# Hybrid decoder block: part of the first modulation summed by column products, and tile 1 of x moved to a later load

## What is computed

```python
c_act = jax.nn.silu(c)
mod = (c_act @ w_ada[l] + b_ada[l])[:, None, :]
sh1, sc1, g1, sh2, sc2, g2 = jnp.split(mod, N_MOD, axis=-1)
h = rms_norm(h_res, norm1_g[l]) * (1.0 + sc1) + sh1
proj = h @ w_in[l]                       # q | k | v | u, width 1280
# q, k: QK-norm and partial rotary; sliding-window attention with sinks
# u: pooling mixer over windows of 2, 4, 8 and 16 positions
h_res = h_res + g1 * mixed
h2 = rms_norm(h_res, norm2_g[l]) * (1.0 + sc2) + sh2
ff = jnp.square(jax.nn.relu(h2 @ w_mlp_in[l])) @ w_mlp_out[l]
h_res = h_res + g2 * ff
```

## Time and profile before

| | us |
|---|---|
| median of 3 runs | 965.35 (964.99 to 967.53) |
| the profiled execution | 964.76 |
| its span between first and last instruction | 963.0 |
| PE busy | 923.1 |
| DVE busy | 656.4 |
| ACT busy | 491.4 |
| POOL busy | 348.6 |

### The profile page before, as it was taken

How to read it: one execution, slowest core, us unless ns; L and a number is a source line. 1 busy time by engine, 2 the same in 40 slices (tenths; PEclk the granted TensorE clock), 3 DMA queues, 4 the chain that set the end, 5 groups by cost and what they waited for, 6 DMA issues and landing times.

```text
span 963.0 us, 12639 instructions
## 1 busy us (share of the span) xinstructions
PE 923.1 (96%) x4411; PEld 762.8 (79%) x4411; DVE 656.4 (68%) x1000; ACT 491.4 (51%) x874; POOL 348.6 (36%) x342
## 2 busy tenths in 40 slices
PE   1899999998999999999999999999999999999998
PEld 1787788886778888788888788888888888888887
DVE  6976887878554587665566544535687666789896
ACT  1756677778465564645544455454343544333331
POOL 8041211116232443988788877851000000000000
PEclk9999999999999999999999999999999999999999
DMA  9852432214222240765456534548998837997772
GB/s 357 323 170 74 131 110 88 80 54 155 87 88 88 88 153 22 232 203 177 164 168 203 176 132 134 173 143 274 331 354 292 280 98 235 312 323 233 237 248 105
DMA packets 92271, 175.54 MB, mean 182 GB/s; under 512 B 9320, under 2 KB 26288, under 8 KB 92208
## 3 DMA queue, kind: packets, MB, share of 16 engines
q1 hardware_dynamic: 92096, 174.70, 54.0%
q10 hardware_dynamic: 112, 0.04, 0.0%
HBM read 136.95 MB, written 37.75 MB: 181 GB/s over the span
## 4 chain that ended last, share of the span: by engine, by line
PE 84%; DVE 7%; ACT 5%; issue 2%; DMA 1%; SPq 1%; POOL 0%; DVEq 0%; ACTq 0%
PE psum L1965 26%; PE psum L1967 26%; PE psum L1966 25%; PE psum L1961 3%; DMA slots<-in_w_ada 1%; ACT probs L777 1%; PE psum L2041 1%; ACT qT L796 1%; DVE squares L1162 1%; PE psum L2091 1%; PE psum L2022 1%; PE psum L2020 1%; PE psum L2019 1%; ACT probs L785 1%; PE psum L2064 1%
## 5 line engine op out<-in xcount | busy, mean ns | idle before, releaser
L1072 ACT CAST down_operands<-down_raw 128x1024 fp32r<-128x1024 f32 x96 | 100.9, 1054 | 152.5 <-PE psum L1967 57.6
L1965 PE MATMUL psum<-down_operands 128*128 128x512 f32 x448 | 174.3, 389 | 0.0
L1966 PE MATMUL psum<-down_operands 128*128 128x512 f32 x448 | 174.3, 389 | 0.0
L1967 PE MATMUL psum<-down_operands 128*128 128x512 f32 x448 | 174.3, 389 | 0.0
L1701 DVE TENSOR_TENSOR down_operands<-down_raw,down_operands 128x1024 fp32r<-128x1024 f32 x93 | 112.4, 1220 | 16.3 <-ACT down_operands L1072 15.4
L1965 PE MATMUL psum<-h2T,w_operands 128*128 128x512 f32 x272 | 107.4, 395 | 1.9 <-DVE act_quads_a L1645 1.3
L1967 PE MATMUL psum<-h2T,w_operands 128*128 128x512 f32 x272 | 106.0, 390 | 0.0
L1966 PE MATMUL psum<-h2T,w_operands 128*128 128x512 f32 x272 | 105.9, 389 | 0.0
L1917 POOL TENSOR_TENSOR w_operands<-raw,w_operands 128x512 fp32r<-128x512 f32 x56 | 83.1, 1485 | 42.2 <-ACT w_operands L1024 42.2
L1966 PEld LDWEIGHTS psum<-down_operands 128*128 128x128 f32 x448 | 84.1, 188 | 17.6
L1965 PEld LDWEIGHTS psum<-down_operands 128*128 128x128 f32 x448 | 84.1, 188 | 17.5
(11 more groups left out here) (249 smaller groups left out, 1965.5 us busy)
## 6 DMA issues: line engine op xcount, KB each, us to landing
down_raw<-in_w_mlp_out SPq DMA_DIRECT2D x160, 256.0 KB, 4.5
down_raw<-act_scratch SPq DMA_DIRECT2D x112, 256.0 KB, 3.4
raw<-in_w_ada SPq DMA_DIRECT2D x32, 512.0 KB, 4.5
raw<-in_w_mlp_in SPq DMA_DIRECT2D x32, 512.0 KB, 4.8
act_scratch<-act_quads_a SPq DMA_DIRECT2D x64, 256.0 KB, 2.3
act_scratch<-act_quads_b SPq DMA_DIRECT2D x48, 256.0 KB, 3.5
slots<-in_w_ada SPq DMA_DIRECT2D x8, 512.0 KB, 10.5
xh<-in_x SPq DMA_DIRECT2D x8, 512.0 KB, 5.8
```

The source lines that it names most:

```text
L1072: nc.scalar.copy(o[:, 0, :, :], r[:, 0:2, :]).then_inc(op2_hi, 1)
L1965: mm(o, wh, ah, start=first, stop=False, skip_group_check=adds)
L1966: mm(o, wh, al, start=False, stop=False, skip_group_check=adds)
L1967: return mm(o, wl, ah, start=False, stop=last, skip_group_check=adds)
```

## The change

- sc1 pieces 6 and 7 are no longer added by DVE (`SC1_DVE` is KD - 2, which is 6). PE multiplies them directly: `column_sum` takes 128 columns of the piece as the stationary operand and one column as the moving operand (silu for a raw piece, ones for a sum that DVE has made), which sums over the partitions and lands the result as one column of PSUM. acc is summed in that way too, and acc_sc (pieces 0 to 5), all of sc1 into the same PSUM columns. `turn_sums` and the three `TENSOR_REDUCE` go.
- Tile 1 of x is issued behind wu piece 1 instead of ahead of sc1, squared on ACT behind `hi_wu(1)`, scaled on GpSimd (`g.tensor_scalar` on `xh[:, 1, :]`) and turned behind `project_u(0)`.
- The six `keep_clock` products between the turns of x and of acc_sc go.
- The buffers of sc1 pieces 6 and 7 are given back by PE (`sc1_used`, `sc1_turned`).

```diff
@@ the buffers of sc1
-                eng.wait_ge(mod_summed, k + 1 + (KD if kind == "sc1" else 0) + (kind == "sc1" and k == KD - 1))
+                if kind == "sc1" and k == SC1_DVE:
+                    eng.wait_ge(sc1_used, 1)
+                elif kind == "sc1" and k == KD - 1:
+                    eng.wait_ge(sc1_turned, 2)
+                else:
+                    eng.wait_ge(mod_summed, k + 1 + (KD if kind == "sc1" else 0))
@@ SP
-                if n == 7:
+                if n == place[("sh1", KD - 1)]:
                     load_x(0)
+                if n == place[("wu", 1)]:
                     load_x(1)
@@ ACT
             square_x(0)
-            square_x(1)
             scale_x(0)
-            scale_x(1)
             hi_wu(0)
             hi_wu(1)
+            square_x(1)
             hi_h(0, 0)
@@ DVE
-            for n in range(2 * KD):
+            for n in range(KD + SC1_DVE):
...
-                    v.tensor_reduce(b1, banks(0).rearrange("p (k n) -> p k n", n=P), AX_X, ALU.add).then_inc(mod_taken, 1)
...
+                    v.tensor_tensor(b1.rearrange("p (h k) -> p h k", h=2), psum[:, 0:2, 0:4],
+                                    cols[:, 8 * SH1:8 * SH1 + 8].rearrange("p (h k) -> p h k", h=2),
+                                    ALU.add).then_inc(mod_taken, 1)
...
-                own_d.step(v.tensor_reduce(a1[:, c4], bank(2 + h).rearrange("p (k n) -> p k n", n=P), AX_X, ALU.add))
-                own_d.wait()
-                own_d.step(v.tensor_tensor(a1[:, c4], a1[:, c4],
+                own_d.step(v.tensor_tensor(a1[:, c4], psum[:, 2 + h, 0:4],
                                            cols[:, 8 * SC1 + 4 * h:8 * SC1 + 4 * h + 4], ALU.add))
@@ GpSimd
-            pool.wait_ge(x_squared, 2)
-            root(rx[:, 0:2], ssx[:, 0:2], D, x_root)
+            root_x(0)
+            root_x(1)
+            pool.wait_ge(x_root, 2)
+            g.tensor_scalar(xh[:, 1, :], xh[:, 1, :], rx[:, 1:2], None, ALU.mult).then_inc(x_scaled, 1)
@@ PE
+            def column_sum(at, n, a, by, first, last):
+                to = psum[:, at + n // 4, n % 4:n % 4 + 1]
+                return mm(to, a[:, n * P:(n + 1) * P], by, start=first and n % 4 == 0, stop=last, skip_group_check=True)
...
-            turn_sums(banks(0), acc).then_inc(mod_turned, 1)
+            for n in range(KD):
+                ins = column_sum(0, n, acc, ones[:, 0:1], True, True)
+            ins.then_inc(mod_turned, 1)
             pe.wait_ge(mod_summed, 2 * KD - 5)
             keep_clock(8, 2)
             turn_x(0)
-            pe.wait_ge(cols_ready, 1)
-            turn_x(1)
-            keep_clock(6, 2)
+            a = landed(pe, ("sc1", SC1_DVE))
+            for n in range(KD):
+                ins = column_sum(2, n, a, silu[:, SC1_DVE:SC1_DVE + 1], True, False)
+            ins.then_inc(sc1_used, 1)
+            pe.wait_ge(mod_summed, KD + SC1_DVE)
+            for n in range(KD):
+                column_sum(2, n, acc_sc, ones[:, 0:1], False, False)
+            a = landed(pe, ("sc1", KD - 1))
             for h in range(2):
-                pe.wait_ge(mod_summed, 2 * KD + h)
-                turn_sums(bank(2 + h), acc_sc[:, 512 * h:512 * h + 512]).then_inc(sc1_turned, 1)
+                for n in range(4 * h, 4 * h + 4):
+                    ins = column_sum(2, n, a, silu[:, KD - 1:KD], False, True)
+                ins.then_inc(sc1_turned, 1)
             pe.wait_ge(mod_taken, 1)
             keep_clock(14, 0)
 
             project_u(0)
+            turn_x(1)
```

More of the change, by code:

```diff
@@ L233, in build @@
         WO_POOL, WO_DVE = (0, 5, 6), (1, 2, 3, 4, 7)
+        SC1_DVE = KD - 2
         JOB_LOADS = (4, 4, 4, 3, 4, 4, 1, 0)
@@ L268, in build @@
         sc1_turned = sem("sc1_turned")
+        sc1_used = sem("sc1_used")
         mod_taken = sem("mod_taken")
@@ L704, in scale_x @@
             def scale_x(t):
-                act.wait_ge(x_root, max(t, 1))
+                act.wait_ge(x_root, t + 1)
                 nc.scalar.activation(xh[:, t % 2, :], xh[:, t % 2, :], ACT.Copy,
@@ L1195, in _ @@
                     add_piece(acc[:, :], ("sh1", n), n, mod_summed)
-                elif n < 2 * KD - 1:
+                else:
                     add_piece(acc_sc, ("sc1", n - KD), n - KD, mod_summed)
-                else:
-                    a = landed(dve, ("sc1", KD - 1))
-                    for h in range(2):
-                        cut = slice(512 * h, 512 * h + 512)
-                        v.scalar_tensor_tensor(out=acc_sc[:, cut], in0=a[:, cut], scalar=silu[:, KD - 1:KD],
-                                               in1=acc_sc[:, cut], op0=ALU.mult, op1=ALU.add).then_inc(mod_summed, 1)
                 if n == 4:
@@ L1206, in _ @@
                     v.tensor_copy(rows[64:72, :], posi[64:72, :]).then_inc(posf_ready, 1)
-                if n == KD + 2:
+                if n == KD - 1:
                     dve.wait_ge(rows_turned, 1)
                     v.tensor_copy(cols[:, :], psum[:, 4, 0:72]).then_inc(cols_ready, 1)
-                if n == 2 * KD - 4:
+                if n == KD + 4:
                     dve.wait_ge(cols_ready, 1)
                     dve.wait_ge(mod_turned, 1)
-                    v.tensor_reduce(b1, banks(0).rearrange("p (k n) -> p k n", n=P), AX_X, ALU.add).then_inc(mod_taken, 1)
-                    dve.wait_ge(mod_taken, 1)
-                    own_d.step(v.tensor_tensor(b1, b1, cols[:, 8 * SH1:8 * SH1 + 8], ALU.add))
+                    v.tensor_tensor(b1.rearrange("p (h k) -> p h k", h=2), psum[:, 0:2, 0:4],
+                                    cols[:, 8 * SH1:8 * SH1 + 8].rearrange("p (h k) -> p h k", h=2),
+                                    ALU.add).then_inc(mod_taken, 1)
             def scale_1(h):
                 c4 = slice(4 * h, 4 * h + 4)
+                if h == 0:
+                    dve.wait_ge(mod_taken, 1)
                 dve.wait_ge(sc1_turned, h + 1)
-                own_d.step(v.tensor_reduce(a1[:, c4], bank(2 + h).rearrange("p (k n) -> p k n", n=P), AX_X, ALU.add))
-                own_d.wait()
-                own_d.step(v.tensor_tensor(a1[:, c4], a1[:, c4],
+                own_d.step(v.tensor_tensor(a1[:, c4], psum[:, 2 + h, 0:4],
                                            cols[:, 8 * SC1 + 4 * h:8 * SC1 + 4 * h + 4], ALU.add))
```

## The result

| | median, us | runs | ratio to before [95%] |
|---|---|---|---|
| before | 965.32 (964.99 to 967.53) | 5 | |
| after | 972.78 (969.17 to 974.13) | 5 | 1.0066 [1.0054, 1.0078] |
| after once more | 973.88 (972.32 to 974.06) | 4 | 1.0078 [1.0063, 1.0093] |

The change loses 7.5 us. The forecast was 967.2, a loss of 1.9, and the range ended at 970.8. The forecast's likeliest case did not happen; its slower rival, TensorE at the lower clock level, did.

A forecast was written before the change was run, and what follows sets the result against it. PE, 96% busy, was bound by when it enters tile 0's projection, set by T plus 16.3 us of DVE work. T +2.5, reduction -0.65: +1.9 on 964.76 gives 966.7, median 967.2; range 963.0 to 970.8.

The forecast's parts named there:

- likeliest case: Late root of tile 0 with PE at its higher clock level: +0.5 to +2.8 us, chance 0.45.
- T: Start of make_h on DVE, 31.60 us before; forecast at 34.1 (33.3 to 34.1), a move of +2.5.
- L: End of DVE's last low part of the weights, 47.93 us before; forecast shift +1.9.
- Root late on POOL: DVE's additions hold small POOL instructions, so the root of tile 0 ends at 25.9 us, against 24.34 before.
- Price of the late root: Without DVE holding POOL, the root would be ready by 21.5 and the forecast sum 1.2 us less.
- Column products: On PE, 40 instructions ahead of a1's first half at 0.11 us: 4.4 us; bounds 2.4 and 9.2.
- Scaling of tile 1 on GpSimd: Begins at 32.2 us, takes 1.90; DVE's second small step of a1 ends with it, giving T = 34.1.
- Behind T: DVE's 16.3 us become 15.65 without the second reduction; turn of tile 1 on PE hidden, cover 0.8 us.
- Rival of the lower level: PE's clock stays low, products 0.17 to 0.23 us, T 36.0 to 38.4: +4.4 to +7, near 970.5; chance 0.22.
- Rival of the cheap products: Root in time on POOL, PE products at 0.11 us or less: 964.6 down to 962 us; chance 0.25.
- Rival of no move: Landing of the weights, not DVE's list, bounds the part behind T: 965.4 us; chance 0.08.

The follow-up runs named there:

- after once more: The changed kernel run again with nothing altered: 973.88 us, ratio 1.0078 to before.
- typical profile: Profile from the unchanged rerun of the changed kernel: span 972.0, time 973.71 us; that run's median is 973.88.
- filled: Changed kernel with keep_clock(18, 2) instead of keep_clock(8, 2), filling PE's pause ahead of the turn of tile 0; products still one column: 969.86 us, ratio 1.0045.
- first profile of after: Profile of the changed kernel's fastest execution of its first five: span 967.4, time 969.17 us.
- the square above: Medians of the changed kernel, late then early root of tile 0: one-column products 973.88 and 967.37 us; 128-column sc1 products 969.08 and 964.14 us.
- x1_only: Kernel before with only tile 1 of x moved (load, square, GpSimd scaling, turn), sums as before: 966.43 us, ratio 1.0008.
- wide_root: Changed kernel with the 24 sc1 products moving 128 columns and the root of tile 0 early on POOL: 964.14 us, ratio 0.9974.
- wide_root_act: Changed kernel with 128-column sc1 products and early root, tile 1 scaled on ACT behind hi_wu(3) instead of GpSimd: 963.87 us, ratio 0.9983.
- wide24: Changed kernel with the 24 products of sc1 moving 128 equal columns instead of one: 969.08 us, ratio 1.0033.
- root_early: Changed kernel with POOL making the root of tile 0 ahead of the fourth pooling window's constants: 967.37 us, ratio 1.0013.
- x1_act_fed: Kernel before with tile 1 moved but scaled on ACT, early root, and keep_clock(24, 0) instead of keep_clock(14, 0): 964.41 us, ratio 0.9979.

## Why the prediction was wrong

**The step that failed** is the term for the column products: 40 instructions at 0.11 us, 4.4 us, with the clock taken to be at its higher level. In the typical profile they run at the lower level, at 0.20 to 0.213 us, and take 8.4 us; PE's `keep_clock(14, 0)` behind them stays at the lower level too, so that the turn of tile 1, which the sum had hidden, comes 2.25 us late. The price is right for the higher level (0.106). What was wrong is that the level would stay. The prediction named this as its first rival and weighed one row against it: the turns at 29.78, at the higher level after 0.49 us of pause. That pause is much shorter than the 2.2 us that the prediction itself expected, and the row has no narrow product in it. PE was as busy as with `keep_clock`, 4.00 of 4.00 us in `filled`, and the clock fell all the same.

The forecast of T, 34.1, redone with what the typical trace shows: the turn starts 0.4 later than thought (27.50) and takes 1.76 instead of 0.9 us, the forty instructions take 8.4 instead of 4.4 us, and the small steps of DVE fall behind the scaling of tile 1 and are not held, which gives 1.06 back. 34.1 + 0.4 + 0.86 + 4.0 - 1.06 = 38.3; the trace has 38.29. So of the 7.1 us between the forecast shift of L (+1.9) and the measured one (+8.98), about 4.2 lie ahead of T and about 3 behind it.

Point by point:

- *Loads*: right. sc1 piece 0 was expected at 17.2; DVE takes it at 16.8 in the typical trace and at 17.8 in the other.
- *Root late on POOL*: the end of the root was right in the typical trace, 26.26 against the forecast 25.9, and so were the idle PE ahead of the turn (3.26 us, 2.2 forecast) and that DVE's additions hold small GpSimd instructions up. But that the number fits is luck in part. The count began with a memset at 18.4 and six instructions behind it, one per addition. In the typical trace that memset comes at 21.39, as the constants ahead of it were held up already; of the six behind it three were held and three slipped through once DVE was done:

```profile
21.57 0.90 POOL L1786 TENSOR_SCALAR_AFFINE_SELECT band<-band 128x16 f32<-128x16 f32 x1
...
25.70 0.56 POOL L1823 TENSOR_TENSOR small<-small 128x1 f32<-128x1 f32 x1
```

  In the first profile of after the memset comes at 18.20, as the prediction had it. There two selections slipped through around a pause of DVE (18.69 to 19.06) and the root ended at 24.73, not at 25.9. Timeline of POOL in that profile:

```profile
23.13 1.60 POOL L1823 TENSOR_TENSOR small<-small 128x1 f32<-128x1 f32 x1
...
32.85 2.86 POOL L1832 TENSOR_SCALAR xh<-xh,small 128x1024 f32<-128x1024 f32 x1
```

  The instruction that takes 1.60 us here takes 0.56 at 25.70 in the typical profile, when DVE is done with its additions. That is what the Trainium skill's "SBUF — State Buffer", section "SBUF: two separate sides", would have: whichever of the two starts first holds the shared ports for its whole length.
- *Price of the late root*: the square above gives 4.9 to 6.5 us. The prediction put it at 1.2 us, which doesn't follow from its own terms either: 2.2 us for the turn and 1.05 for the scaling, less up to 0.7 further on, is 2.5. It priced the delay alone, without what stands at the lower level behind it.
- *Column products*: the mechanism of the price (the weight load) was right, the size only for one level. The Trainium skill's "TensorE: Matmul & The Clock Gate", section "LDWEIGHTS (loading the stationary operand)", gives columns / 1.2 in ns, 107 ns here. The traces agree at the higher level (0.106) and not at the lower, where it is 0.213. The bounds 0.06 and 0.23 held both.
- *Scaling of tile 1 on GpSimd*: mis-sized, 2.86 us instead of 1.90. That it holds one of DVE's small steps was right where the two meet: 0.53 us in the first profile of after, 0.66 in `x1_only`, 0.83 in `wide_root`, against 0.16 in `wide_root_act`. That the step ends with the scaling was wrong. It ends 1.12 to 1.13 us behind the scaling's start in all three (33.98, 33.27 and 33.31, the scaling from 32.85, 32.14 and 32.18), with another 1.7 us of scaling to come, and the splitting of a weight, which has two inputs in SBUF, then runs at its usual 1.22 us beside it (33.38 in `x1_only`). So the rule of the whole length holds in these rows for GpSimd behind DVE and is not borne out for DVE behind GpSimd, unless the scaling's recorded length is too long; no run tells the two apart. Held to the end of the scaling, T in the first profile would be near 35.75. In the typical run they don't meet.
- *T in the first profile*, 34.02, agrees with the forecast 34.1 only by chance: the root was 1.2 us early there, the turn of tile 0 ran at the lower level (1.62 us instead of 0.9), and so did the last ten or so of the forty instructions.
- *Behind T*: wrong. From T to L 15.65 us were forecast; it is 17.25 in the first profile of after and 18.62 in the typical one. The removed reduction is there, but the turn of tile 1, said to be hidden with 0.8 us to spare, comes 0.9 and 2.25 us late (DVE reached it at 43.10 before, so 10.8 us behind T without the reduction and not 11.1: the cover was about 0.5 thin), and 0.6 us more are lost at the last low parts, half of it in a wait for an ACT high part. With wide products the cover holds: no such wait in `wide24` and `wide_root`, whose T to L is 15.83 and 16.39, the latter with the 0.83 us step in it.
- *Rival of the lower level*: this is what happened. It asked for products at 0.17 to 0.23 us and T at 36.0 to 38.4 (measured 0.20 to 0.213 and 38.29), and a sum of +4.4 to +7; measured +7.5. (Its T leaves out the 0.2 us ahead of DVE's steps that the sum has; with them it is 36.2 to 38.6.) It had a chance of 0.22, and the range was cut at 970.8, inside it. Its "another 1 us from the cover" was too little by its own terms: 28 instructions at 0.23 are 3.1 us longer than 3.3, and a cover of 0.8 leaves 2.3. Measured are waits of 2.07 to 2.32 us in the three traces where `keep_clock(14, 0)` takes 5.6 to 6.0 us (`root_early`, typical, `filled`).
- *Rival of the cheap products*: 0.06 us or below an instruction was seen nowhere; the lowest is 0.106.
- *Rival of no move*: excluded; the shift of L is the shift of the time in eight of the thirteen profiles, within 0.2 us, and the other five have more time at the lower clock.

What stays open: what made sc1 piece 0 come 1.0 us later, and POOL's last memset 3.2 us earlier, in one execution of after than in another, of which one pauses 3.26 us ahead of the turn and the other 0.46; and why the clock falls at some 225 to 240 us in some executions of several kernels only. In the first profile of after that fall comes behind two pauses of PE, of 1.11 and 0.72 us (PE is busy 1.16 of the 2.00 us from 226); before has such a pause too (0.89 of 2.00 us from 222) and no fall.

## What to carry to other kernels

An engine that the profile calls busy isn't yet one that keeps its clock. Where small TensorE products stand ahead of a critical stretch, price them at both clock levels, and price what stands behind them at the lower one too. Where such products are bound by their weight load anyway, let them move 128 columns instead of one: here that cost 0.112 instead of 0.106 us an instruction, and more room in PSUM, and the clock rose and stayed up. And a chain with time to spare (here the root on POOL) must be looked at again when a change puts the critical work behind it in the same queue.

## What was not expected of the hardware

- A column product in float32 costs 0.106 us an instruction at the higher level and 0.213 at the lower. With 128 moved columns it is 0.112 at the higher level.
- PE with 24 narrow products (48 instructions) in a row is busy without a gap, and the granted clock falls to 0.50 before they are through (`filled`, 33.3 us). The Trainium skill's "TensorE: Matmul & The Clock Gate", section "HAM oscillation — how this bites in real kernels", tells of clocks that fall in PE's waits for data; here the clock fell without one.
- GpSimd's scaling of 128x1024 float32 by a column took 2.85 to 2.86 us in every trace that has it, ACT's 1.15. A small DVE step with two inputs in SBUF that met it was held until 1.13 us behind the start of the scaling, and no longer.
- A stretch at 0.50 of 3.4 us, far from the change, went with an end 1.1 to 1.2 us later than the shift of L in `x1_only`, `x1_act_fed` and the first profile of after.
